# Attention of a two-layer decode-and-prompt kernel: 32-column tiles for the prompt's values, paged values and paged scores in one run

## The chip, the cores and the metric

One core of one Trainium2 chip. The time is that of one launch on the device, in microseconds (us); lower is better. A run's number is the time of one execution; three runs are given for the kernel before.

## The reference, cut to what matters

Two layers of a trunk over 1024 prompt tokens and 8 decoding sequences of 4 tokens each. Each layer projects, attends, gates, and then has a feed-forward part. The change touches the attention alone:

```python
def latent_attention(q_abs, q_pe, c_kv, k_pe, q_pos, k_pos, w_uv):
    s = (jnp.einsum('bqhc,bkc->bhqk', q_abs, c_kv)
         + jnp.einsum('bqhr,bkr->bhqk', q_pe, k_pe)) * ATTN_SCALE
    s = jnp.where((k_pos[None, :] <= q_pos[:, None])[None, None], s, NEG_INF)
    p = jax.nn.softmax(s, axis=-1)
    o_lat = jnp.einsum('bhqk,bkc->bqhc', p, c_kv)
    return jnp.einsum('bqhc,chv->bqhv', o_lat, w_uv)
# prompt: 8 blocks of 128 queries, 8 heads, keys up to the own block, 64 values per head
# sample: 8 sequences, each with 4096 cached (paged) positions of 128 latents + 32 rotary numbers,
#         plus its own 4 new positions
```

## The kernel before, in words

All engines run programs of their own that meet in counting semaphores. In each layer the attention is one loop over 64 "halves" `i`, written out on each engine. Half `i` is one head (`e = i % 2`) of job `k = i // 2`; `JOBS[k]` is a pair `(u, j)`: pair of heads `u`, query block `j` with `j + 1` key blocks of 128. For `u` = 0, 1, 2 the blocks come in the order 0, 7, 1, 6, 2, 5, 3, 4; for `u` = 3 as 4, 3, 5, 2, 6, 1, 7, 0. Four halves make a step `c = i // 4`, and `ph = i % 4` is the half within the step. "First half" is `ph` 0 and "third half" `ph` 2. A half with `j >= 4` is called big: its scores take two PSUM banks and its transposed probabilities two ring entries.

The prompt's part of a half, engine by engine:

- TensorE: `scores` of half `i + 2` into banks 0 to 3 (L2618, with the mask in L2621), `turn_p` transposes the normalised probabilities of half `i`, 128 columns at a time (L2630), and at the start of every second half `values(k - 1)` multiplies values by the transposed probabilities of the finished job (L2644), 64 columns of weights for each head, in bank 6.
- VectorE: `maxima` (L1898, the row maxima of the scores of half `i + 2`), `normalise` (L1904, L1907), `take_pt` (L1921, copies the second ring entry of a big half), `take_o` (L1914).
- ScalarE: `exps` (L1174), `take_pt` (L1187, copies the first ring entry of a half), `take_o` (L1181, the high part of the job's output).

One step of the paged part is laid between the four halves. Step `c` treats 512 cached positions of four sequences: `turn_keys` transposes the latents (L2665, two blocks in `ph` 0, two in `ph` 1; ScalarE L1193 and VectorE L1927 copy them out), VectorE's `take_ropes` (L1934) transposes the rotary keys, `step_scores` (L2676 in 32-column tiles, then L2678 over all columns) writes bank 7, VectorE's `step_max` (L1964) and ScalarE's `step_exp` (L1209) turn it into probabilities, `step_turn` transposes them (L2690), ScalarE's `step_pt` (L1216) copies them, `step_values` multiplies them with the latents (L2701, in 32-column tiles, bank 6), and VectorE's `step_out` (L1983) adds to the running sum. Every eighth step a short part for the new positions comes in (`new_scores`, `new_turn`, `new_values`, L2728). The latents arrive by SyncE's DMAs into three buffers, and a buffer's next DMAs wait for the `step_values` that read it.

The transposes go through a ring of two PSUM banks (4 and 5) in one order fixed by `ring_table`; entry `n` may be written when entry `n - 2` has been copied out (`evicted`), and ScalarE and VectorE must copy in that order too. The order on TensorE before is: `ph` 0: values, transposes, scores, keys, then `step_values(c - 1)`; `ph` 2: values, transposes, scores, then `step_scores(c)`; end of `ph` 3: `step_turn(c)`, except in the two steps for which `short(c)` holds, where it stands behind the next `values`. Because output of prompt and pages shares bank 6's first 128 columns, each writer of the bank waits for the readers of the one before (`o_new`, `do_free`).

## Time and profile before

| what | before |
|---|---|
| median of 3 runs | 2509.25 us (2505.19 to 2509.54) |
| profiled execution, first to last instruction | 2500.6 us |
| TensorE matmul busy | 2445.4 us, 98% |
| TensorE weight load busy | 2197.3 us, 88% |
| VectorE, ScalarE busy | 1527.6 us (61%), 1025.4 us (41%) |
| granted TensorE clock | 0.997 |

The profiled execution is known by its span alone, 2500.6 us; the median of the runs lies 8.65 us above it. A busy matmul engine in this profile is one with a matmul in its pipeline: a lone matmul of 128 columns counts 0.27 us, while in a stream the next starts 0.03 to 0.11 us after it. Time lost on TensorE therefore shows best in the distance between starts. Each fp32 matmul with real weights appears as two records, a transpose as one.

### The profile page before, as it was taken

The numbers are of one execution on the slowest core, as the hardware profiler recorded it, in microseconds if no ns is written. First come the engines' busy times: TensorE is split into PE (matmuls) and PEld (weight loads), VectorE is DVE, ScalarE is ACT, GpSimd is POOL, SyncE is SP. The second block draws the span as 40 slices with busy tenths as digits, with TensorE's granted clock in tenths as the row PEclk, the third lists the DMA queues.
The fourth block names the chain that finished last, engine by engine and source line by source line (L and its number), as shares of the span: only waits on it lengthen the run. The fifth ranks groups of instructions, "written<-read, shape, count | busy, mean of one in ns | idle before, by whom it ended". The sixth has DMA issues, their size and how long they took to land.

```text
span 2500.6 us, 47127 instructions
## 1 busy us (share of the span) xinstructions
PE 2445.4 (98%) x18500; PEld 2197.3 (88%) x18500; DVE 1527.6 (61%) x1986; ACT 1025.4 (41%) x1535; POOL 926.5 (37%) x395
## 2 busy tenths in 40 slices
PE   8999999999999999999999999999999999999998
PEld 6996666897999999999979966668989999999998
DVE  5546666348776557655674566663497675567646
ACT  3224555327533333433441246552274333333334
POOL 2331000122664666455213310002136654665451
PEclk9999999999999999999999999999999999999999
DMA  6114322314545544663431143222236356445644
GB/s 224 55 39 119 94 86 81 119 59 149 199 161 213 204 157 152 214 217 142 148 113 50 35 130 89 87 87 109 75 126 252 145 182 232 165 151 180 223 141 154
DMA packets 182347, 347.40 MB, mean 139 GB/s; under 512 B 33969, under 2 KB 46449, under 8 KB 181425
## 3 DMA queue, kind: packets, MB, share of 16 engines
q1 hardware_dynamic: 116128, 207.12, 24.9%
q10 hardware_dynamic: 63504, 129.77, 14.3%
q0 software_dynamic: 2560, 8.39, 1.2%
q8 instruction: 105, 1.72, 0.3%
q14 instruction: 50, 0.40, 0.1%
HBM read 292.94 MB, written 49.06 MB: 137 GB/s over the span
## 4 chain that ended last, share of the span: by engine, by line
PE 81%; DVE 7%; ACT 4%; POOLq 3%; issue 2%; DVEq 1%; DMA 1%; POOL 1%; SPq 0%; ACTq 0%
PE psum L2926 21%; PE psum L2973 20%; PE psum L2428 12%; PE psum L2618 4%; PE psum L2413 3%; PE psum L2644 3%; PE psum L2458 3%; PE psum L2630 2%; PE psum L2521 2%; PE psum L2665 2%; PE psum L2477 2%; PE psum L2381 1%; ACT z L1174 1%; PE psum L2488 1%; PE psum L2678 1%
## 5 line engine op out<-in xcount | busy, mean ns | idle before, releaser
L2973 PE MATMUL psum<-hidh,wh 128*128 128x264 f32 x1312 | 374.2, 285 | 8.4 <-issue 5.9
L2973 PE MATMUL psum<-hidl,wh 128*128 128x264 f32 x1312 | 373.6, 285 | 0.0
L2973 PE MATMUL psum<-hidh,wl 128*128 128x264 f32 x1312 | 372.7, 284 | 0.0
L2926 PE MATMUL psum<-hh,wh 128*128 128x264 f32 x1280 | 363.4, 284 | 0.1
L2926 PE MATMUL psum<-hh,wl 128*128 128x264 f32 x1280 | 362.8, 283 | 0.0
L2926 PE MATMUL psum<-hl,wh 128*128 128x264 f32 x1280 | 362.6, 283 | 0.0
L2134 DVE TENSOR_TENSOR z<-psum,z 128x528 f32<-128x528 f32 x336 | 226.9, 700 | 94.1 <-PE psum L2973 94.1
L2973 PEld LDWEIGHTS psum<-hidh,wh 128*128 128x128 f32 x1312 | 246.5, 188 | 10.4 <-issue 7.0
L2973 PEld LDWEIGHTS psum<-hidh,wl 128*128 128x128 f32 x1312 | 247.2, 188 | 0.0
L2973 PEld LDWEIGHTS psum<-hidl,wh 128*128 128x128 f32 x1312 | 246.9, 188 | 0.0
L2926 PEld LDWEIGHTS psum<-hh,wh 128*128 128x128 f32 x1280 | 240.5, 188 | 0.5 <-issue 0.5
L2926 PEld LDWEIGHTS psum<-hh,wl 128*128 128x128 f32 x1280 | 240.6, 188 | 0.0
L2926 PEld LDWEIGHTS psum<-hl,wh 128*128 128x128 f32 x1280 | 240.5, 188 | 0.0
L2428 PE MATMUL psum<-hh,wh 128*128 128x352 f32 x720 | 234.7, 326 | 0.1
L2428 PE MATMUL psum<-hh,wl 128*128 128x352 f32 x720 | 231.4, 321 | 0.0
L2428 PE MATMUL psum<-hl,wh 128*128 128x352 f32 x720 | 231.0, 321 | 0.0
L792 POOL TENSOR_TENSOR wh<-raw,ones 128x1024 fp32r<-128x1024 f32 x36 | 72.3, 2007 | 347.2 <-PE psum L2428 259.4
L808 POOL TENSOR_TENSOR wl<-raw,wh 128x1024 fp32r<-128x1024 f32 x42 | 108.3, 2579 | 181.3 <-ACT wh L1354 178.3
L904 POOL DMA_INDIRECT z<-cache_k,krows x32 | 30.5, 954 | 379.5 <-DVE cn L1934 375.2
L2124 DVE TENSOR_TENSOR hidl<-z,hidh 128x1056 fp32r<-128x1056 f32 (+1 forms) x100 | 159.1, 1591 | 10.4 <-ACT hidh L1340 10.4
L808 POOL TENSOR_TENSOR wl<-sacc,wh 128x1024 fp32r<-128x1024 f32 x38 | 92.3, 2428 | 146.8 <-ACT wh L1354 127.7
L2428 PEld LDWEIGHTS psum<-hh,wh 128*128 128x128 f32 x720 | 135.1, 188 | 2.1 <-DVE hl L1709 0.7
(329 smaller groups left out, 5935.0 us busy)
## 6 DMA issues: line engine op xcount, KB each, us to landing
hh<-h_quarters ACTq DMA_DIRECT2D x60, 1056.0 KB, 5.4
hl<-h_quarters ACTq DMA_DIRECT2D x60, 1056.0 KB, 7.5
raw<-wst SPq DMA_DIRECT2D x48, 512.0 KB, 3.6
z<-cache_c SPq DMA_DIRECT2D x352, 64.0 KB, 1.8
x<-x_spill SPq DMA_DIRECT2D x4, 4224.0 KB, 14.5
sacc<-wst SPq DMA_DIRECT2D x56, 256.0 KB, 3.2
t<-wst SPq DMA_DIRECT2D x56, 256.0 KB, 3.0
cn<-wst SPq DMA_DIRECT2D x56, 256.0 KB, 3.9
```

Of the source, the lines that this page charges most:

```text
L792: pool.tensor_tensor(wh[:, s, :], src, ones[:, 0:1].to_broadcast([P, TW]), ALU.mult)
L808: pool.tensor_tensor(wl[:, s, :], src, wh[:, s, :].bitcast(F32), ALU.subtract).then_inc(split.sem, 1)
L2124: dve.tensor_tensor(hid_of(t, hidl)[:, ks, :], src[:, ks, :], hid_of(t, hidh)[:, ks, :].bitcast(F32), ALU.subtract).then_inc(hid_l.sem, 1)
L2134: dve.tensor_tensor(part, dn_banks(u), part, ALU.add).then_inc(dn_free.sem, 1)
L2413: ins = pe.matmul(bank3(u, g), w, m[:, k, cols(g)], start=(first and n == 0), stop=(last and n == 2))
L2428: ins = pe.matmul(bank3(u, g), w[:, s, o:o + P], m[:, k, cols(g)], start=(k == 0 and n == 0), stop=(k == kk - 1 and n == 2))
L2458: ins = pe.matmul(bank, u_w[w], m[:, k, cols(g)], start=(first and n == 0), stop=(last and n == 2))
L2477: ins = pe.matmul(bank3(u, g), nxt[u][:, k * P:k * P + P], x[:, k, cols(g)], start=(k == 0), stop=(k == KD - 1))
L2618: ins = pe.matmul(ps[2 * e + h][:, 0:w], qs[e][0:KQ, u, tok(j)], keys[0:KQ, 2 * (u % 2) + e, 512 * h:512 * h + w], start=True, stop=not last)
L2644: ins = pe.matmul(ps[6][64 * e:64 * e + 64, 0:P], vals[:, kb, (2 * u + e) * VD:(2 * u + e) * VD + VD], pts[2 * e + kb // 4][:, kb % 4, :], ...
L2926: ins = pe.matmul(psum[:, up_bank(st, u) + q, 0:HW], w[:, o:o + P], m[part], start=(fresh and k == 0 and n == 0), stop=(k == 3 and n == 2) ...
L2973: ins = pe.matmul(psum[:, 2 * u + q, 0:HW], w[:, o:o + P], m[:, t, k * HB + q * HW:k * HB + q * HW + HW], start=(fresh and k == 0 and n == ...
```

## The change

It does four things.

- `values` uses four 32-column tiles where it had two of 64; twice as many matmuls, each half as wide in its weights.
- Prompt output, paged output and the output for the new positions get columns of their own in bank 6 (`prompt_o`, `paged_o`, `new_o`), so TensorE no longer waits for `o_new` or `do_free` before `step_values`, and ScalarE's `take_o` waits in the third half for the paged values' end before it reads the bank. The new positions' probabilities get a place of their own (`ptn`).
- On TensorE the third half now starts with `values`, `step_values(c - 1)`, (`new_values`) and `step_scores(c)` in one run, ahead of the half's transposes and scores. On VectorE the third half's order becomes `normalise(i + 1)`, `take_o`, `step_out(c - 1)`, `step_max(c)`, `take_pt(i)`, `maxima(i + 2)`.
- `step_turn(c - 1)` always stands in the first half, behind `values`; `short` is gone. The ring's entry for it and ScalarE's `step_pt` move with it.

```diff
--- before.py
+++ after.py
@@ -103,6 +103,8 @@
     for i in range(HALVES):
         ph, c = i % 4, i // 4
         big = JOBS[i // 2][1] >= 4
+        if ph == 0 and c > 0:
+            order.append((("x", c - 1), "act"))
         order.append((("p", i, 0), "act"))
         if big:
             order.append((("p", i, 1), "dve"))
@@ -115,7 +117,8 @@
         if ph == 3:
             if i in K_AT:
                 order.append((("k",) + K_AT[i], "act" if K_AT[i][1] == 0 else "dve"))
-            order.append((("x", c), "act"))
+            if c == STEPS - 1:
+                order.append((("x", c), "act"))
             if c == CHUNKS:
                 order.append((("f", 0), "act"))
     table, done = [], {"act": 0, "dve": 0}
@@ -268,6 +271,7 @@
         ptd = cnf[:, 512:1024].rearrange("p (r n) -> p r n", r=4)
         oacc = [zf[:, 9856:9984], cnf[:, 1024:1152]]
         olat = [cnf[:, 1152:1280], zf[:, 0:128]]
+        ptn = olat[0][0:NS, :]
         cks = [f.rearrange("p (b r c) -> p b r c", b=QB, r=4)
                for f in (zf[:, 4224:6272], raw[:, :, :].rearrange("p s n -> p (s n)"), zf[:, 6784:8832])]
         tab = rinv[0:1, 512:768].bitcast(I32).rearrange("o (n q) -> o n q", q=4)
@@ -279,6 +283,7 @@
 
         psum = ctx.enter_context(nc.psum_tensor("psum", [P, 8, 512], F32))
         ps = [psum[:, i, :] for i in range(8)]
+        prompt_o, paged_o, new_o = ps[6][:, 0:P], ps[6][:, P:2 * P], ps[6][:, 2 * P:3 * P]
 
         S = {}
 
@@ -1178,7 +1183,9 @@
 
                     u, j = JOBS[k]
                     act.wait_ge(o_full.sem, at.value(o_full, k + 1))
-                    act.activation(hh[:, u, tok(j)], ps[6][:, 0:P], ACT.Copy).then_inc(o_hi.sem, 1)
+                    if k % 2 == 0:
+                        act.wait_ge(do_full.sem, at.value(do_full, out_of_step(k // 2) - 1))
+                    act.activation(hh[:, u, tok(j)], prompt_o, ACT.Copy).then_inc(o_hi.sem, 1)
 
                 def take_pt(i):
 
@@ -1200,7 +1207,7 @@
 
                 def new_pt(quad):
                     turned(("n", quad))
-                    act.activation(ptd[0:NS, 0, :], ring_bank(("n", quad))[0:NS, 0:P], ACT.Copy).then_inc(t_act.sem, 1)
+                    act.activation(ptn, ring_bank(("n", quad))[0:NS, 0:P], ACT.Copy).then_inc(t_act.sem, 1)
 
                 def step_exp(c):
 
@@ -1248,6 +1255,8 @@
                         exps(i + 1)
                     if i % 2 == 0 and k > 0:
                         take_o(k - 1)
+                    if ph == 0 and c > 0:
+                        step_pt(c - 1)
                     take_pt(i)
                     if ph == 0:
                         take_keys(c, 0)
@@ -1264,7 +1273,8 @@
                         step_exp(c)
                         if i in K_AT and K_AT[i][1] == 0:
                             more_keys(K_AT[i][0])
-                        step_pt(c)
+                        if c == STEPS - 1:
+                            step_pt(c)
                         if c == CHUNKS:
                             turned(("f", 0))
                             act.activation(olat[0], ring_bank(("f", 0))[:, 0:P], ACT.Copy).then_inc(t_act.sem, 1)
@@ -1911,7 +1921,7 @@
 
                     u, j = JOBS[k]
                     dve.wait_ge(o_hi.sem, at.value(o_hi, k + 1))
-                    dve.tensor_tensor(hl[:, u, tok(j)], ps[6][:, 0:P], hh[:, u, tok(j)].bitcast(F32),
+                    dve.tensor_tensor(hl[:, u, tok(j)], prompt_o, hh[:, u, tok(j)].bitcast(F32),
                                       ALU.subtract).then_inc(o_new.sem, 1)
 
                 def take_pt(i):
@@ -1954,7 +1964,7 @@
                     dve.wait_ge(dexp.sem, at.value(dexp, first))
                     dve.tensor_copy(stat[:, 23:24], stat[:, 14:15])
                     dve.wait_ge(do_full.sem, at.value(do_full, first))
-                    dve.tensor_copy(oacc[quad], ps[6][:, 0:P]).then_inc(do_free.sem, 1)
+                    dve.tensor_copy(oacc[quad], new_o).then_inc(do_free.sem, 1)
                     dve.drain()
 
                 def step_max(c):
@@ -1981,12 +1991,13 @@
                     quad = c // CHUNKS
                     dve.wait_ge(do_full.sem, at.value(do_full, out_of_step(c)))
                     dve.scalar_tensor_tensor(out=oacc[quad], in0=oacc[quad], scalar=stat[:, 6 + s:7 + s],
-                                             in1=ps[6][:, 0:P], op0=ALU.mult, op1=ALU.add).then_inc(do_free.sem, 1)
+                                             in1=paged_o, op0=ALU.mult, op1=ALU.add).then_inc(do_free.sem, 1)
                     dve.drain()
                     if c % CHUNKS == CHUNKS - 1:
                         dve.reciprocal(stat[:, 22:23], stat[:, 23:24])
                         dve.drain()
                         dve.tensor_scalar(oacc[quad], oacc[quad], stat[:, 22:23], None, ALU.mult).then_inc(on_new.sem, 1)
+                        dve.drain()
 
                 gate_low(NB)
                 dve.wait_ge(vs_out.sem, at.value(vs_out, 16))
@@ -2007,11 +2018,17 @@
                 for i in range(HALVES):
                     k, ph, c = i // 2, i % 4, i // 4
                     big = JOBS[k][1] >= 4
+                    if ph == 2:
+                        normalise(i + 1)
                     if i % 2 == 0 and k > 0:
                         take_o(k - 1)
+                    if ph == 2:
+                        if c > 0:
+                            step_out(c - 1)
+                        step_max(c)
                     if big:
                         take_pt(i)
-                    if i + 1 < HALVES:
+                    if ph != 2 and i + 1 < HALVES:
                         normalise(i + 1)
                     if ph == 0 and c > 0:
                         take_ropes(c)
@@ -2022,13 +2039,9 @@
                             take_ropes(c)
                     if i + 2 < HALVES:
                         maxima(i + 2)
-                    if ph == 0:
-                        if c > 0:
-                            step_out(c - 1)
-                        if c % CHUNKS == 0:
-                            new_max(c // CHUNKS)
+                    if ph == 0 and c % CHUNKS == 0:
+                        new_max(c // CHUNKS)
                     if ph == 2:
-                        step_max(c)
                         if c % CHUNKS == 0:
                             new_out(c // CHUNKS)
                     if ph == 3:
@@ -2641,10 +2654,10 @@
                     pe.wait_ge(do_free.sem, at.value(do_free))
                     for kb in range(j + 1):
                         for e in range(2):
-                            ins = pe.matmul(ps[6][64 * e:64 * e + 64, 0:P],
-                                            vals[:, kb, (2 * u + e) * VD:(2 * u + e) * VD + VD],
-                                            pts[2 * e + kb // 4][:, kb % 4, :], start=(kb == 0), stop=(kb == j),
-                                            skip_group_check=True, tile_position=(0, 64 * e))
+                            for v in (64 * e, 64 * e + 32):
+                                ins = pe.matmul(prompt_o[v:v + 32, :], vals[:, kb, 2 * u * VD + v:2 * u * VD + v + 32],
+                                                pts[2 * e + kb // 4][:, kb % 4, :], start=(kb == 0), stop=(kb == j),
+                                                skip_group_check=True, tile_position=(0, v))
                     ins.then_inc(o_full.sem, 1)
                     at.step(o_new)
 
@@ -2678,10 +2691,6 @@
                     pe.matmul(ps[7][:, :], qrd[:, quad, :], rtt, start=False, stop=True,
                               skip_group_check=True).then_inc(ds_full.sem, 1)
 
-                def short(c):
-
-                    return c < STEPS - 1 and JOBS[2 * c + 1][1] + JOBS[2 * c + 2][1] < 7
-
                 def step_turn(c):
 
                     pe.wait_ge(dexp.sem, at.value(dexp, c + c // CHUNKS + 2))
@@ -2694,11 +2703,9 @@
 
                     s = c % CBUFS
                     evicted(RING_AT["x", c])
-                    pe.wait_ge(o_new.sem, at.value(o_new))
-                    pe.wait_ge(do_free.sem, at.value(do_free))
                     for r in range(4):
                         for b in range(QB):
-                            ins = pe.matmul(ps[6][rows_of(b), 0:P], ptd[:, r, rows_of(b)], cks[s][:, b, r, :],
+                            ins = pe.matmul(paged_o[rows_of(b), :], ptd[:, r, rows_of(b)], cks[s][:, b, r, :],
                                             start=(r == 0), stop=(r == 3), skip_group_check=True,
                                             tile_position=(0, 32 * b))
                     ins.then_inc(do_full.sem, 1)
@@ -2724,8 +2731,7 @@
 
                 def new_values(quad):
                     evicted(RING_AT["n", quad])
-                    pe.wait_ge(o_new.sem, at.value(o_new))
-                    pe.matmul(ps[6][:, 0:P], ptd[0:NS, 0, :], cn[0:NS, NB, 0:CL], start=True,
+                    pe.matmul(new_o, ptn, cn[0:NS, NB, 0:CL], start=True,
                               stop=True).then_inc(do_full.sem, 1)
                     at.step(do_free)
 
@@ -2774,8 +2780,14 @@
                     next_big = i + 2 < HALVES and JOBS[k + 1][1] >= 4
                     if i % 2 == 0 and k > 0:
                         values(k - 1)
-                    if ph == 0 and c > 0 and short(c - 1):
+                    if ph == 0 and c > 0:
                         step_turn(c - 1)
+                    if ph == 2:
+                        if c > 0:
+                            step_values(c - 1)
+                        if c % CHUNKS == 0:
+                            new_values(c // CHUNKS)
+                        step_scores(c)
                     turn_p(i, 0)
                     if i + 2 < HALVES:
                         scores(i + 2, 0)
@@ -2789,18 +2801,12 @@
                         scores(i + 2, 1)
                     if ph == 0:
                         turn_keys(c, 1)
-                        if c > 0:
-                            step_values(c - 1)
                         if c % CHUNKS == 0:
                             new_scores(c // CHUNKS)
                     if ph == 1:
                         turn_keys(c, 3)
                         if c % CHUNKS == 0:
                             new_turn(c // CHUNKS)
-                    if ph == 2:
-                        step_scores(c)
-                        if c % CHUNKS == 0:
-                            new_values(c // CHUNKS)
                     if ph == 3:
                         if i in K_AT:
                             u, h = K_AT[i]
@@ -2812,7 +2818,7 @@
                             pe.wait_ge(exped.sem, at.value(exped, HALVES))
                             pe.wait_ge(gate_l.sem, at.value(gate_l, NB + 1))
                             out_part(0, (4, 5, 6, 7))
-                        if not short(c):
+                        if c == STEPS - 1:
                             step_turn(c)
                         if c == CHUNKS:
                             pe.wait_ge(on_new.sem, at.value(on_new, 1))
@@ -2825,6 +2831,8 @@
                 evicted(len(RING) - 2)
                 evicted(len(RING) - 1)
                 out_part(1, (4, 5))
+                pe.wait_ge(o_new.sem, at.value(o_new))
+                pe.wait_ge(do_free.sem, at.value(do_free))
                 step_values(STEPS - 1)
                 out_part(1, (6, 7))
                 pe.wait_ge(on_new.sem, at.value(on_new, 2))
```

## Rows read from the trace of the kernel before

**Rows 1.** The page: busy time, share of the span, instructions.

```profile
PE 2445.4 (98%) x18500; PEld 2197.3 (88%) x18500; DVE 1527.6 (61%) x1986; ACT 1025.4 (41%) x1535; POOL 926.5 (37%) x395
```

**Rows 2.** Busy time by stretch, us and instructions: the first layer's attention.

```profile
core 0: us, PE busy (x) PEld busy (x) DVE busy (x) ACT busy (x) POOL busy (x), PEclk, DMA share, GB/s
215.00:465.00 250.00, 241.97 (x2139) 160.87 (x2138) 162.10 (x385) 144.42 (x350) 12.31 (x13) 1.00 0.30 88
```

**Rows 3.** Timeline of step 6, third half to values: start, us, engine, line.

```profile
321.18 0.38 PE L2630 MATMUL psum<-cst,z 128*128 128x128 f32 x2
...
321.49 1.07 PE L2676 MATMUL psum<-z,sacc 128*32 128x512 f32 x8
321.60 0.43 DVE L1921 COPY t<-psum 128x256 f32<-128x256 f32 x1 [0.40 <-PE psum L2630]
...
322.17 0.62 DVE L1907 TENSOR_SCALAR z<-z,stat 128x768 f32<-128x768 f32 x1
322.49 1.13 PE L2678 MATMUL psum<-cn,sacc 128*128 128x512 f32 x2
322.71 0.68 DVE L1898 TENSOR_REDUCE stat<-psum 128x1 f32<-128x512 f32 x1
...
323.43 0.69 ACT L1174 ACTIVATE z<-psum,stat 128x512 f32<-128x512 f32 x1 [2.06 <-DVE stat L1898]
323.45 0.60 PE L2630 MATMUL psum<-cst,z 128*128 128x128 f32 x4
...
323.89 1.02 PE L2618 MATMUL psum<-scratch,free_b 96*128 96x512 f32 x2
...
324.11 0.59 ACT L1187 ACTIVATE t<-psum 128x512 f32<-128x512 f32 x1
...
324.81 0.38 PE L2630 MATMUL psum<-cst,z 128*128 128x128 f32 x2
...
325.23 0.42 DVE L1921 COPY t<-psum 128x256 f32<-128x256 f32 x1 [0.66 <-PE psum L2630]
...
325.44 0.66 PE L2690 MATMUL psum<-cst,z 128*128 128x128 f32 x4 [0.25 <-ACT z L1209]
...
326.03 1.53 PE L2644 MATMUL psum<-t,scratch 128*64 128x128 f32 x24
```

**Rows 4.** Timeline behind those values.

```profile
327.49 0.66 PE L2630 MATMUL psum<-cst,z 128*128 128x128 f32 x4
```

**Rows 5.** Timeline around the paged values of step 4.

```profile
299.30 0.60 PE L2665 MATMUL psum<-cst,z 128*128 128x128 f32 x4
...
299.83 1.08 PE L2701 MATMUL psum<-raw,cn 128*32 128x128 f32 x32
...
300.85 0.44 PE L2630 MATMUL psum<-cst,z 128*128 128x128 f32 x2
```

**Rows 6.** Timeline at the end of step 7, one of the two short ones.

```profile
338.48 0.30 PE L2630 MATMUL psum<-cst,z 128*128 128x128 f32 x1
...
338.81 0.29 DVE L1921 COPY t<-psum 128x128 f32<-128x128 f32 x1
...
339.43 0.19 PEld L2644 LDWEIGHTS psum<-t,scratch 128*64 128x64 f32 x3 [0.85 <-ACT t L1187]
```

**Rows 7.** TensorE's waits of the whole run; one wait of step 4.

```profile
PEld psum L2690 <- ACT z L1209: 13.9, 26, 0.8
PEld psum L2630 <- DVE z L1907: 7.5, 16, 1.4
...
292.09 0.42 PEld L2630 LDWEIGHTS psum<-cst,z 128*128 128x128 f32 x4 [1.40 <-DVE z L1907]
```

**Rows 8.** Timeline of step 6, second half: a copy and the key transpose behind it.

```profile
316.83 0.49 ACT L1187 ACTIVATE t<-psum 128x384 f32<-128x384 f32 x1
...
318.36 0.42 PEld L2665 LDWEIGHTS psum<-cst,z 128*128 128x128 f32 x4
```

**Rows 9.** Timeline of step 12, second half: the same pair.

```profile
409.64 0.59 ACT L1187 ACTIVATE t<-psum 128x512 f32<-128x512 f32 x1
...
410.28 1.09 PE L2665 MATMUL psum<-cst,z 128*128 128x128 f32 x8 [0.29 <-ACT t L1187]
```

## The prediction, made before the changed kernel was seen

> **What bounds the kernel now.** I read the page first: the matmul engine shows 98% of the span, VectorE 61%, ScalarE 41% [rows 1]. Nearly all of the gain or loss must be time on TensorE. The change touches only the attention, so I then took the first layer's attention by stretch: TensorE 242.0 of 250 us, VectorE 162.1, ScalarE 144.4, clock at its full level of 2.4 GHz [rows 2]. The second layer's is the same program. "Busy" hides small losses here, because a matmul of 128 columns counts 0.27 us while the next may start 0.11 us later. So I read the timeline by distances between starts. In a stream of transposes it is 0.11 us ((0.60 - 0.27) / 3 of the four records at 323.45 [rows 3]); anything longer is a mode switch or a wait.
>
> In step 6 the order of events is [rows 3]: the last third-half transposes at 321.18, the paged scores 321.49 to about 323.45, then the fourth half's transposes and scores, a wait for ScalarE, the paged transposes at 325.44, the values at 326.03. TensorE is in a stream throughout except for one wait of 0.41 us: the two transposes at 324.81 leave it free at 325.03, and the next starts at 325.44. So TensorE sets the pace, but its neighbours are close behind: the copy that the values need ended at 325.65 (325.23 + 0.42), 0.38 us before they started. What lies between a transposition and the values that use it is therefore not spare.
>
> **Gains, both layers.**
>
> *Mode switches.* Full to 32-column tiles: the last of the four key transposes starts at 299.63, the first paged value matmul at 299.83, 0.203 us instead of 0.110 [rows 5]. Into and out of the 64-column tiles it is the same: 1.53 us for 24 records puts the last start at 327.29, the next is at 327.49 [rows 3, 4]. I price a switch at 0.093 us. The third half had four switches besides the one inside the paged scores (in and out of values, into the scores), the paged values two in the first half. In one run, two of the former vanish in each of 16 steps and both of the latter in 15, less two where the new positions' scores stay; 60 a layer, 120 x 0.093 = 11.2 us.
>
> The Trainium skill ("TensorEngine Tiling (Array Packing)", Key Properties) says that changing the tiling mode drains the engine. Read as a full drain of 0.27 us, a switch would cost 0.163 us more than a stream and 120 of them 19.6 us; the sum below would end 8 us lower. The trace shows 0.093, before the last matmul's end, so I keep that.
>
> *Narrower values.* A 64-column record takes (1.53 - 0.27) / 23 = 54.8 ns [rows 3], a 32-column one (1.08 - 0.27) / 31 = 26.1 ns [rows 5]. A key block needs 4 of the former (219 ns) or 8 of the latter (209 ns): 144 blocks a layer, 288 x 0.0104 = 3.0 us. The four tiles run side by side just as the two did; no stream is halved.
>
> *Waits that go.* The paged transposes waited for the exponential. Summed over weight loads this is 13.9 us in 26 places [rows 7], but a weight load may start early; by distances between starts, as above, I get 0.41 us in step 6 and between 0 and 0.66 in the others, 6.7 in all (bounds 3.5 and 13.9). Both short steps of a layer wait before the values: the last transpose could be followed at 338.68 by a switched stream, the load starts at 339.43 [rows 6]; 4 x 0.78 = 3.1. In step 4 the fourth half's transposes wait for `normalise` [rows 7]; it now stands first on VectorE. That and its like in step 0 give about 2.6. Together 12.4 us.
>
> Gains: 11.2 + 3.0 + 12.4 = 26.6 us.
>
> **Costs, both layers.**
>
> *The values of every second job, at the head of the first half.* This is the large term. `step_scores` stood between the score matmuls of the next step's first half and the fourth half; `step_turn` stood between the fourth half's transposes and the values. Both covers go. What the values need is the fourth half's first ring entry, copied by ScalarE, and ScalarE copies it behind `exps` of the next half, which waits for VectorE's `maxima`, which stands behind `take_pt` of the third half. From the end of the third half's last transpose (321.56) that chain costs, in durations of rows 3: copy 0.35 (0.43, with 0.08 overlapped), maxima 0.68, exponential 0.68 (323.43 to 324.11), copy 0.59, and three hand-overs of 0.04: 2.42 us. TensorE's own work until the values is what ran from 323.45 to 325.03, 1.58 us, counted from 0.16 us before that end, plus one switch of 0.09: 1.51 us. So it stands 0.9 us. Then come the remaining waits in front of `values`: in step 7 the copy ends at 339.10 and the load starts at 339.43 [rows 6], 0.33 us later, where a single wait costs 0.05 (the exponential's in rows 3). I take 0.2: 1.1 us.
>
> From the other side: the short steps already lack `step_turn` in front of the values and wait 0.78 us with only one block to copy in the second entry (0.29 us); with four blocks, 0.39 more. VectorE's copy alone thus gives 0.78 to 1.17 us. In steps 0, 4 and 8 the third half has eight blocks, its `normalise` ends late and pushes `step_max` and the copy back; there I estimate 1.4 to 1.5. In the steps where keys are made in the fourth half that matmul waits instead of the values, for the same entry. For the last pair of heads, whose third halves are small, the same chain from the maxima gives about 0.95. Average 1.1, bounds 0.78 and 1.5. Fifteen boundaries a layer: 30 x 1.1 = 33 us. This replaces the two kinds of waits counted above as gone.
>
> *The second half.* Without the paged values (1.02 + 0.09 = 1.11 us of TensorE, rows 5) in the first half, the key transposes reach their ring entry sooner. In step 6 the copy ends at 317.32 and the fourth key transposition starts at 318.36: slack 1.04, lost 1.11 [rows 8]. Steps with fewer blocks in the third half have less slack; I estimate 0.1 to 0.4 us, 11 steps a layer at 0.17: 3.8 us. In steps 12 to 15 there is no slack: the copy ends at 410.23, the transposes start at 410.28 after 0.46 us of waiting [rows 9], and the chain behind it (copy, normalise, the rotary transposition, maxima, exponential, copy) starts at the first half's transposes, which the run does not delay. The full 1.11 is lost: 8 x 1.1 = 8.8 us (bounds 4 and 9). `new_values` now stands ahead of the scores and waits for its copy: 2 x 0.5 = 1.0.
>
> Costs: 33 + 3.8 + 8.8 + 1.0 = 46.6 us. Costed at nothing: `step_exp` in the fourth half (the paged transposes come two blocks of work later); ScalarE's extra wait in `take_o` (its next copy belongs to transposes that come after the run anyway); the gathers, which are released by `step_values` two halves later but have a step and a half left before use. If that cover failed, the first key transposes of a step would wait for a DMA.
>
> **The sum.** 46.6 - 26.6 = +20.0 us on 2500.6, so a span of 2520.6. The runs' median is 8.65 above the span: 2529.
>
> **Rivals.**
>
> 1. *The copies come in time*: faster. Place: the wait before the values at the head of the first half. With no wait there the sum is 13.6 - 26.6 = -13.0 (2496); with 0.2 us each, -7 (2502). It decides at 0.43 us a boundary. For it: VectorE and ScalarE are a third idle [rows 2], and both have less queued behind the run. Against it: idle engines do not shorten a chain of latencies, and rows 6 show 0.78 with more cover. 0.13.
>
> 2. *Nothing measurable*, the same wait at 0.3 to 0.55 us: 0.08.
>
> 3. *The chain grows*: `step_max` and `step_out` hold VectorE up in most steps as in steps 0, 4, 8, so that a boundary costs 1.5 us: +12 us more, 2541. For it: the paged scores' last matmul counts 0.6 us after its start and VectorE must wait for it. Against it: in steps with seven blocks or fewer the next transposes and scores cover this. 0.11.
>
> 4. *Narrow tiles stream faster*: 13 ns a record instead of 26 would save 288 x 0.104 = 30 us more, 2499. Rows 5 show 26.1 with the same moving width. 0.01. The Trainium skill ("TensorEngine Tiling (Array Packing)", Theoretical Speedup) lists up to 2x for 64 and up to 4x for 32, which taken for the prompt's values would say this; here the narrower tile also halves the work of each matmul.
>
> 5. The forecast, 0.67.
>
> **How the numbers follow.** About 0.2% (5 us) is what a measurement of this kernel tells from no change. Faster: rivals 1 and 4, 0.14. Same: 0.08. Slower: the rest, 0.78. The forecast's own bounds (0.78 to 1.5 us a boundary, 4 to 9 in the last steps) reach from 2515 to 2541. To leave out no more than 2 in 10 the range takes in rival 2, the edge of rival 1 and rival 3 with some spread: 2504 to 2545.
>
> **What the changed profile would show.** Right: the first values matmul of each first half stands idle about 1 us behind ScalarE L1187 or VectorE L1921; the wait for the exponential before the paged transposes is gone; values, paged values and paged scores follow each other at 0.03 us; VectorE's key-side waits in steps 12 to 15 grow. Wrong: idle time before those values under 0.4 us; or a wait on the gathers; or a 32-column run of a hundred records that streams slower than 26 ns, which would add to the loss instead.

## The result and the profile after

The changed kernel takes 2529.59 us (median of 4, 2528.96 to 2530.73) against 2507.22 us before (4, 2501.65 to 2509.54): ratio 1.0088, 95% interval 1.0074 to 1.0102. It is slower by 22 us. The forecast was 2529 us.

The page after, to be read beside [rows 1], and the first layer's attention by stretch, beside [rows 2] (the stretch is 10 us longer, because the attention is):

```profile
PE 2437.0 (96%) x19652; PEld 2204.6 (87%) x19652; DVE 1531.3 (61%) x1986; ACT 1024.6 (41%) x1535; POOL 923.6 (37%) x395
```

```profile
core 0: us, PE busy (x) PEld busy (x) DVE busy (x) ACT busy (x) POOL busy (x), PEclk, DMA share, GB/s
215.00:475.00 260.00, 236.29 (x2701) 161.96 (x2700) 162.85 (x384) 143.74 (x349) 12.23 (x13) 0.99 0.31 86
```

VectorE and ScalarE do what they did. TensorE is busy for less time (236.3 instead of 242.0 us), but it stands 23.7 us idle instead of 8.0. The granted clock was 0.99 of full after and 1.00 before. So the loss is waiting, and the question is for what.

I measure the attention of a layer as the distance between the first transposition of its first half and that of its last. Before, it is 241.62 and 242.28 us, 483.90 in both layers; after, 252.42 and 252.09, 504.51. That is +20.6 us. The groups of the transposition line after, by source line, show the two ends roughly (the last half's block itself is included):

```profile
L2643 PE MATMUL psum<-cst,z x288: 270/273/468, 221.8 to 474.3; 128*128 128x128 f32 x144
...
L2643 PE MATMUL psum<-cst,z x288: 270/273/468, 1474.7 to 1726.7; 128*128 128x128 f32 x144
```

The waits of the weight loads over the whole run (us in total, times, longest), which answer to [rows 7]:

```profile
PEld psum L2658 <- ACT t L1194: 24.8, 22, 1.4
...
PEld psum L2579 <- ACT t L1194: 8.9, 8, 1.2
...
PEld psum L2643 <- ACT cn L1223: 7.0, 6, 1.9
...
PEld psum L2643 <- DVE t L1931: 2.9, 4, 0.9
```

The paged transposition's 13.9 us behind the exponential have shrunk to 0.9 us in four places. In their place stand 24.8 us before the prompt's values (22 places) and 8.9 us before the key-making matmul (8 places), both for the copy `take_pt`: together 30 places, the 30 boundaries of the forecast. The third row, 7.0 us in six places, was not forecast: the first half's own transposes wait for a ring entry that `step_pt` has not copied yet. The fourth, 2.9 us in four places, is in the fourth half of steps 0 and 4, where the transposes wait for VectorE's copy.

Step 6 after, in the timeline (start, us, engine, line), beside [rows 3, 4]:

```profile
321.23 0.86 PE L2658 MATMUL psum<-t,scratch 128*32 128x128 f32 x24
...
321.91 1.06 PE L2708 MATMUL psum<-z,cn 128*32 128x128 f32 x32
...
322.78 1.04 PE L2689 MATMUL psum<-z,sacc 128*32 128x512 f32 x8
...
323.75 1.12 PE L2691 MATMUL psum<-cn,sacc 128*128 128x512 f32 x2
...
324.71 0.60 PE L2643 MATMUL psum<-cst,z 128*128 128x128 f32 x4
...
326.50 0.42 DVE L1931 COPY t<-psum 128x256 f32<-128x256 f32 x1 [0.55 <-PE psum L2643]
...
326.84 0.68 DVE L1908 TENSOR_REDUCE stat<-psum 128x1 f32<-128x512 f32 x1
...
327.55 0.69 ACT L1179 ACTIVATE z<-psum,stat 128x512 f32<-128x512 f32 x1 [1.60 <-DVE stat L1908]
327.65 0.39 PE L2643 MATMUL psum<-cst,z 128*128 128x128 f32 x2
...
328.08 0.42 DVE L1931 COPY t<-psum 128x256 f32<-128x256 f32 x1 [0.56 <-PE psum L2643]
...
328.23 0.59 ACT L1194 ACTIVATE t<-psum 128x512 f32<-128x512 f32 x1
...
329.02 1.52 PE L2658 MATMUL psum<-t,scratch 128*32 128x128 f32 x48 [0.98 <-ACT t L1194]
...
330.47 0.66 PE L2699 MATMUL psum<-cst,z 128*128 128x128 f32 x4
```

The forecast chain can be read off: copy of the third half 326.50, maxima 326.84, exponential 327.55, ScalarE's copy 328.23 to 328.82, values 329.02. TensorE's last transpose before them starts at 327.76 (327.65 + 0.11); a switched stream would have started the values at 327.96. The wait is 1.06 us.

### The profile page after: what moved, and what is told of

It is laid out like the page before. It is cut to its first block, busy times and chain, and to the rows that moved or that the text cites. A ratio compares the mean times of both kernels' runs of the same rounds, so it can differ in the third digit from the quotient of the medians.

```text
span 2527.2 us, 49433 instructions
## 1 busy us (share of the span) xinstructions
PE 2437.0 (96%) x19652; PEld 2204.6 (87%) x19652; DVE 1531.3 (61%) x1986; ACT 1024.6 (41%) x1535; POOL 923.6 (37%) x395
## 4 chain that ended last, share of the span: by engine, by line
PE 79%; DVE 8%; ACT 4%; issue 3%; POOLq 2%; DVEq 1%; POOL 1%; DMA 1%; SPq 0%; ACTq 0%
PE psum L2934 20%; PE psum L2981 19%; PE psum L2441 12%; PE psum L2471 3%; PE psum L2426 3%; PE psum L2631 3%; PE psum L2658 2%; DVE stat L1908 2%; PE psum L2534 2%; ACT z L1179 2%; PE psum L2490 2%; PE psum L2678 1%; PE psum L2643 1%; PE psum L2394 1%; PE psum L2691 1%
```

## The experiments

For each, "attention" is the sum over both layers as above (before 483.9, after 504.5). Outside the attention the profiled runs spread over 2016.7 to 2028.1 us, in kernels that are the same there. So a difference of a few microseconds between two spans is read from the attention. It is that of one profiled execution for each kernel; its two layers agree within 0.8 us in every kernel.

### e1: only the narrower values, in the kernel before

```diff
-                            ins = pe.matmul(ps[6][64 * e:64 * e + 64, 0:P],
-                                            vals[:, kb, (2 * u + e) * VD:(2 * u + e) * VD + VD],
+                            for v in (64 * e, 64 * e + 32):
+                                ins = pe.matmul(ps[6][v:v + 32, 0:P], vals[:, kb, 2 * u * VD + v:2 * u * VD + v + 32],
...
-                                            skip_group_check=True, tile_position=(0, 64 * e))
+                                                skip_group_check=True, tile_position=(0, v))
```

> The kernel before with the prompt's values in 32-column tiles and nothing else. Measured over the two attention stretches (first transposition of half 0 to that of half 63; 483.9 us together before, 504.5 in the changed kernel). Theory (the order costs, the tiles give a little): 3.0 us less, about 481, no new wait. Rival (twice as many value matmuls cost issue time or instruction loading): 484 or more, a 32-column record slower than 26 ns in the long streams.

Measured: 2508.14 us, ratio 0.9989 (0.9978 to 1.0000), attention 484.39. Most steps became 0.01 to 0.03 us shorter. Step 8 rose by 0.7 us in the first layer, in the wait before `new_turn`, and by 0.5 in the second. So the sum rose by 0.5 us where 3.0 less was expected. A narrow record takes 26.5 ns in a long stream (1.245 us for the 47 intervals of 48 records) where the wide one takes 54.8. Two narrow for one wide gain 1.8 ns, not the 2.6 that I had taken from the short run of [rows 5]. And a block of values has one more interval to pay, since the hand-over behind it stays at 0.203 us: 24 wide records took 1.258 us from first to last, 48 narrow ones 1.245. Over 32 steps this is about 1 us.

### e2: the changed kernel with the 64-column values back

```diff
-                            for v in (64 * e, 64 * e + 32):
-                                ins = pe.matmul(prompt_o[v:v + 32, :], vals[:, kb, 2 * u * VD + v:2 * u * VD + v + 32],
...
+                            ins = pe.matmul(ps[6][64 * e:64 * e + 64, 0:P],
+                                            vals[:, kb, (2 * u + e) * VD:(2 * u + e) * VD + VD],
...
```

> The changed kernel with 64-column tiles for the prompt's values; the order is kept. Theory: slower than the changed kernel by 3.0 us of stream and one more switch in each of 32 third halves (0.093 less the hand-over within the run, 1 to 3 us): stretches about 509. Rival (the narrow tiles cost): below 504.

Measured: 2534.06 us (one run), attention 506.99, so +2.5 (+4 to +6 was expected). Steps 0 to 14 rose by 3.6 us together, up to 0.17 each, and the last step fell by 0.5 and 0.6; why it fell no experiment shows. Within the run, equal tiles are worth little: one switch saved a step, and a part of that comes back at the hand-over (last section).

### e3: the paged scores back behind the third half

```diff
                             new_values(c // CHUNKS)
-                        step_scores(c)
                     turn_p(i, 0)
...
+                    if ph == 2:
+                        step_scores(c)
```

VectorE's `step_max` goes back behind `maxima` with them.

> The changed kernel with the paged scores back at the end of the third half (VectorE's step_max behind maxima again); values and paged values still run together at its head. Theory (the values at the head of the first half lost their cover): the wait before them, 0.8 to 1.2 us at 30 boundaries and 29.6 us in all, falls to near nothing, two switches in each of 32 steps come back (5 to 6 us): stretches about 480, 20 to 24 below the changed kernel. Rival (the moved paged transposition is what uncovers the values): the wait stays over 0.6 us a boundary, stretches about 500.

Measured: 2519.84 us, ratio 1.0038 (1.0024 to 1.0052), attention 491.87: 12.6 us less than the changed kernel, not the 20 to 24 expected. The wait vanished in steps 12 to 14 and in three of the four that make keys (5, 8, 9), but stayed in step 4 (0.84 us) and in seven others a layer. Step 6 of this kernel in the timeline shows who ends it now:

```profile
320.59 1.12 PE L2691 MATMUL psum<-cn,sacc 128*128 128x512 f32 x2
...
322.19 0.60 ACT L1194 ACTIVATE t<-psum 128x512 f32<-128x512 f32 x1 [0.36 <-PE psum L2643]
...
322.91 0.38 PE L2643 MATMUL psum<-cst,z 128*128 128x128 f32 x2
...
323.33 0.42 DVE L1931 COPY t<-psum 128x256 f32<-128x256 f32 x1 [0.66 <-PE psum L2643]
...
324.12 1.52 PE L2658 MATMUL psum<-t,scratch 128*32 128x128 f32 x48 [0.83 <-DVE t L1931]
```

ScalarE's copy is in time (322.79), as I had argued. VectorE's copy of the second entry is not: it can't start before the two transposes just ahead of the values end. From the last of these starts (323.02) to the values it takes 1.10 us, of which 0.20 is a stream. This floor of 0.9 us has nothing to do with the scores: it stands in e7 and e10 too, where they are at their old place. The paged transposition used to hide it, and it is what moving the transposition costs wherever the second entry has nothing else behind it. The scores' part is what went: between nothing and 0.2 us in steps 1 to 3, 6, 7 and 10, 0.35 in step 11, and the whole 0.9 to 1.2 in steps 5, 8 and 9 and in steps 12 to 14. In step 0 the wait even grew (1.16 to 1.47 us). And 4.8 of the 12.6 us went elsewhere, in the fourth half's transposes of steps 0, 4, 3 and 7 (see the section on why the prediction was right).

### e4: e3, and the paged transposition home as well

```diff
-                        if c == STEPS - 1:
+                        if not short(c):
                             step_turn(c)
```

with its ring entry and `step_pt` back in the fourth half.

> As e3, and the paged transposition back at the end of the fourth half as before. Theory: the wait for the exponential returns (6.7 us by distances before), the ring waits of the last pair of heads behind the paged entry go (some 5 us): stretches within 3 us of e3. Rival (moved transposition is the loss): 15 us or more below e3.

Measured: 2513.99 us, ratio 1.0019 (1.0009 to 1.0028), attention 487.98: 3.9 us below e3, a little more than the 3 expected; the rival's 15 is far off. What is left of the change here (values run behind each other, narrow tiles, regions of their own, `normalise` first) still stands 4 us above the kernel before. By steps it gains in the plain ones (14.77 and 14.74 us in steps 2 and 6 for 14.98 and 14.95) and loses in steps 12 to 15 (16.54, 16.18, 16.12, 11.64 for 15.42, 15.38, 15.41, 11.19), where the second half was already short of TensorE work; its key transposes wait 1.28 us in step 12, for 0.46 before.

### e10: the opposite, only the paged transposition moved

```diff
-                    if ph == 0 and c > 0 and short(c - 1):
+                    if ph == 0 and c > 0:
                         step_turn(c - 1)
```

in the kernel before, with the ring entry and `step_pt` moved along.

> The kernel before with the paged transposition behind the first half's values, its ring entry and ScalarE's copy moved with it as in the change, and nothing else (in e7 ScalarE's copy stayed ahead of the next exps and held it up). Theory: in steps 1, 2, 6 and 10 a wait of about 0.9 us for VectorE's copy takes the place of 0.4 us for the exponential, so these are 0.4 to 0.5 us longer than before; steps 3 and 7 as before; steps with key making and steps 12 to 15 within 0.3 us: stretches 486 to 491 against 483.9. Rival (moving the transposition is most of the change's loss): 497 or more, as e7.

Measured: 2511.66 us (one run), attention 489.22, +5.3, inside the 486 to 491 expected. Steps 1, 2, 6 and 10 lose 0.45 us each in the first layer, as expected. Steps 14 and 15 lose 0.8 and 0.9, against the 0.3 expected, and step 8 gains 0.9: a wait of 0.92 us between the paged transposition and an extra one that this step has is gone. This kernel has the unforecast wait too, by the weight loads' list:

```profile
PEld psum L2636 <- ACT cn L1219: 5.3, 6, 1.5
```

So it comes from the transposition's new place and not from the run. The floor of e3 can be read here by size: from the last transpose to the values it takes 0.99, 1.10, 1.23 and 1.365 us where VectorE copies one, two, three and four blocks (steps 3, 6, 1, 0). The changed kernel has 0.99, 1.26, 1.42 and 1.365 there, so in these steps the chain over maxima and exponential adds at most 0.2 us to what VectorE's copy takes by itself.

### e6: ScalarE copies before the next exponential

```diff
-                    if 0 < i < HALVES - 1:
+                    if 0 < i < HALVES - 1 and ph != 3:
                         exps(i + 1)
...
                     take_pt(i)
+                    if i < HALVES - 1 and ph == 3:
+                        exps(i + 1)
```

In the changed kernel, this takes maxima and exponential out of the chain in front of the values.

> The changed kernel with one thing other on ScalarE: in the fourth half take_pt stands ahead of the next half's exps. Theory (the values wait for the copy behind exps): the wait before the values of the first half falls from about 1.05 to about 0.85 us where the third half has six or seven blocks (there VectorE's copy of the second entry comes next), and to 0.3 or less at steps 12 to 15, where there is no second entry; stretches 8 to 11 us below the changed kernel's 504.5. Rival (VectorE alone sets the wait): less than 3 us.

Measured: 2518.37 us (one run), attention 496.62, 7.9 us below the changed kernel, at the edge of the 8 to 11 expected. In step 6 the same floor appears as in e3:

```profile
323.38 0.38 PE L2645 MATMUL psum<-cst,z 128*128 128x128 f32 x2
...
323.79 0.42 DVE L1933 COPY t<-psum 128x256 f32<-128x256 f32 x1 [0.56 <-PE psum L2645]
...
324.58 0.86 PE L2660 MATMUL psum<-t,scratch 128*32 128x128 f32 x24 [0.82 <-DVE t L1933]
```

The distance from the last transpose to the values fell from 1.257 to 1.097 us and no further. In steps 12 to 14 the wait was gone, but steps 13 and 14 grew all the same (17.26 and 18.20 us for 16.94 and 17.93): the first half's second group of transposes now waits 1.13 and 1.65 us where it waited 0.25 and 1.10, behind the later exponential.

### e7: the transposition behind the values, but its copy at the old place

```diff
-                    return c < STEPS - 1 and JOBS[2 * c + 1][1] + JOBS[2 * c + 2][1] < 7
+                    return c < STEPS - 1 and c != CHUNKS
```

in the kernel before.

> The kernel before with its paged transposition always behind the first half's values (except at step 8), nothing else of the change. Theory: the wait for the exponential goes (6.7 us) and a wait before the values comes in its place, for VectorE's copy, of 0.7 to 0.9 us in the steps without key making, with no other cover lost: stretches 482 to 490 against 483.9. Rival (this move is the loss of the change): 495 or more.

Measured: 2518.77 us (one run), attention 497.13. A miss by 7 us, and the number of the rival (495 or more). But the wait before the values is the one of e10 (1.10 us from the last transpose in step 6). ScalarE's `step_pt` stayed ahead of the next exponentials and had to wait for a transposition that TensorE now did behind the values, so the exponentials came late: the first half's key transposes of steps 12 to 15 waited 0.9 to 1.35 us, where before they waited 0.1 to 1.05. The moved operation must take its copy with it; that is why e10 costs 5 us and this one 13.

### e8: the paged values back in the first half

```diff
                     if ph == 0:
                         turn_keys(c, 1)
+                        if c > 0 and home(c - 1):
+                            pe.wait_ge(o_new.sem, at.value(o_new))
+                            pe.wait_ge(do_free.sem, at.value(do_free))
+                            step_values(c - 1)
```

in the changed kernel, for every step.

> The changed kernel with the paged values back behind the first half's key transposes; values and paged scores still run together at the head of the third half. Theory: the waits of key transposes and ring in the first and second half fall by the cover of 1.11 us, mostly in steps 12 to 15 (about 8 us), two switches of 0.093 in 30 steps come back (5.6 less two hand-overs of 0.06 each): stretches 2 to 8 us below 504.5, the steps 12 to 15 down by 0.8 each, the others up by 0 to 0.1. Rival (the wait before the values is all of the loss): no step falls.

Measured: 2525.06 us (one run), attention 505.58, +1.1: wrong in sign. Steps 12 to 14 fell by 0.83, 0.78 and 0.74 as expected, so the second half there does miss the paged values. Steps 1, 2, 5, 6, 9 and 10 rose by about 0.5 (step 0 by 0.7 and 0.2, steps 3, 7 and 11 by 0.15 or less, while 4 and 8 fell a little), and the timeline of step 6 shows more in it than two switches:

```profile
321.67 0.86 PE L2665 MATMUL psum<-t,scratch 128*32 128x128 f32 x24
321.77 0.60 ACT L1205 ACTIVATE z<-psum 128x512 f32<-128x512 f32 x1 [1.75 <-PE psum L2685]
...
322.62 0.64 PE L2696 MATMUL psum<-z,sacc 128*32 128x512 f32 x4
```

The paged scores need the step's last keys, whose copy ends at 322.37. With the paged values in front of them, that wait was covered; directly behind the prompt's values the scores come some 0.3 us late, and 0.5 in steps 1, 5 and 9.

### e9: back to the late order where it is better, by step

Transposition home in all steps, scores at the head in steps 0 to 3, 6, 7 and 10 with `step_exp` ahead of `exps`, and paged values home from step 11 on:

```diff
+                    if ph == 3 and head(c):
+                        step_exp(c)
                     if 0 < i < HALVES - 1:
                         exps(i + 1)
```

> A mixture meant to beat both: the paged transposition at the end of the fourth half as before; in steps 0 to 3, 6, 7 and 10 paged scores at the head of the third half with ScalarE's step_exp ahead of exps (it should fit in while ScalarE waits for the maxima); elsewhere paged scores at the end; paged values at home from step 11 on. Theory (cover in front of the values is what counts): the wait there falls to 0.4 to 0.5 us in those seven steps, each about 0.3 us shorter than before; stretches 477 to 482, against 483.9 before. Rival (the exponential delays exps and the chain with it): the seven steps are as long as in the changed kernel, stretches 484 or more.

Measured: 2511.19 us, ratio 1.0015 (1.0004 to 1.0026), attention 485.12: 3 us above the 477 to 482 expected, and in the rival's range (484 or more). The seven steps with the scores at the head are about as long as in the changed kernel. The exponential of the paged scores was early now, but the transposition then waited 0.87 to 1.26 us for the ring entry that `take_pt` frees, because that copy stood behind both exponentials.

### e11: e9 with the copy between the exponentials

```diff
+                    if ph == 3 and head(c):
+                        step_exp(c)
+                    if 0 < i < HALVES - 1 and not (ph == 3 and head(c)):
                         exps(i + 1)
...
                     take_pt(i)
+                    if ph == 3 and head(c):
+                        exps(i + 1)
```

with the scores at the head in steps 0 to 11.

> Meant to beat both. As the changed kernel in steps 0 to 11 with two things other: the paged transposition at the end of the fourth half as before, and ScalarE's order there is step_exp, take_pt, exps; steps 12 to 15 as before. In e9 the transposition waited for the ring entry that take_pt frees behind exps; in e6 the values waited 0.9 us for VectorE's copy with nothing in front. Theory: both go, what is left before the values is 0.3 us; steps 1, 2, 6, 10 at 14.3 to 14.6 us against 14.9 to 15.1 before, stretches 472 to 478 against 483.9, the run some 8 us faster than before. Rival (a later exps uncovers the next chain, or step_exp is too late in ScalarE's order): a new wait at the first half's transposes, stretches 482 or more.

Measured: 2502.41 us against 2507.61, ratio 0.9982 (0.9971 to 0.9992), attention 479.27. It beats both kernels, by 5.2 us and by 27, but is short of what was expected (8 us faster, attention 472 to 478). Its steps 1, 2, 6 and 10 take 14.69, 14.47, 14.47 and 14.52 us (before, steps 1, 2 and 6: 15.09, 14.98, 14.95), at or above the upper end of the 14.3 to 14.6 expected; step 8 even grew, from 18.03 to 18.47. Step 6:

```profile
324.39 0.69 ACT L1223 ACTIVATE z<-psum,stat 128x512 f32<-128x512 f32 x1
...
325.33 0.60 ACT L1201 ACTIVATE t<-psum 128x512 f32<-128x512 f32 x1
...
325.95 0.69 ACT L1186 ACTIVATE z<-psum,stat 128x512 f32<-128x512 f32 x1
326.06 0.38 PE L2657 MATMUL psum<-cst,z 128*128 128x128 f32 x2
...
326.28 0.60 PE L2717 MATMUL psum<-cst,z 128*128 128x128 f32 x4
...
326.48 0.42 DVE L1940 COPY t<-psum 128x256 f32<-128x256 f32 x1 [0.56 <-PE psum L2657]
...
327.26 1.52 PE L2672 MATMUL psum<-t,scratch 128*32 128x128 f32 x48 [0.39 <-DVE t L1940]
```

Paged exponential, copy, next exponential, in this order on ScalarE. The transposition (L2717) stands again between the last two transposes and the values, and of the 0.9 us floor 0.46 is left by the distance between starts. The three-part run is kept, and what it saves is kept with it.

## Why the prediction was right

The moves can be put in a row by their attention time: before 483.9; transposition moved (e10) 489.2; with the values run, narrow tiles and regions (e3) 491.9; with the scores at the head (the change) 504.5. The two moves that took the covers from the values cost 5.3 and 12.6 us. The values standing uncovered is the mechanism of the forecast, and most of both costs. Its terms, measured by distances between starts, both layers:

- **Wait before the values at the head of the first half**: forecast 33 us at 1.1 each, measured 29.8, and 2.6 more one place earlier. In the first layer, less the distance that a stream would have: 1.16, 1.22, 1.05 and 0.79 in steps 0 to 3, 0.9 to 1.2 where keys are made, 1.05 and 0.88 in steps 6 and 7, 1.05 and 0.86 in steps 10 and 11, 0.88 to 0.94 in steps 12 to 14. In steps 0 and 4 VectorE's copy is late behind `step_max`, as forecast, but it is the fourth half's own transposes that wait for it, 0.43 and 0.86 us in each layer. Step 4:

```profile
294.14 0.69 DVE L1931 COPY t<-psum 128x512 f32<-128x512 f32 x1
...
294.88 0.66 PE L2643 MATMUL psum<-cst,z 128*128 128x128 f32 x4 [0.70 <-DVE t L1931]
```

  With it these two steps wait 1.6 and 1.8 us (forecast 1.4 to 1.5), and step 8, where the forecast expected the same, only 0.92. Averaged over 30 boundaries this is 1.08 us, so rival 1 (copies in time), rival 2 (0.3 to 0.55 us) and rival 3 (1.5 us) fall. One thing in the forecast's derivation was off: the chain over maxima and exponential was priced as what the values wait for. e3 and e10 show that in steps 0 to 3, 6, 7 and 10 VectorE's copy alone gives a wait of 0.8 to 1.16 us, which was the forecast's own second estimate, and that the chain ends at most 0.2 us behind it. In steps 5, 8, 9 and 12 to 14, where e3 removed the wait, the chain alone sets it.
- **Second half** (key transposes): forecast 3.8 + 8.8, measured 8.5 in all, about 2 in steps 0 to 11 and 6.5 in the last four. e8 shows its size in steps 12 to 14: about 0.8 us each, not 1.1.
- **The ring**: not in the sum at all, measured 6.7 us (0.25, 1.10 and 1.89 us in steps 13, 14 and 15 of the first layer). This is the step that failed: of the moved transposition I had counted what it no longer covers, and not who waits for the ring entry behind it. In steps 13 to 15 ScalarE reaches `step_pt` only behind a long exponential and `take_o`; the first half's second group of transposes waits. The timeline after, at the last step:

```profile
461.56 1.11 ACT L1179 ACTIVATE z<-psum,stat 128x1024 f32<-128x1024 f32 x1 [1.06 <-DVE stat L1908]
...
462.66 0.27 ACT L1188 ACTIVATE hh<-psum 128x128 fp32r<-128x128 f32 x1
...
462.82 0.60 ACT L1223 ACTIVATE cn<-psum 128x512 f32<-128x512 f32 x1
...
463.47 0.66 PE L2643 MATMUL psum<-cst,z 128*128 128x128 f32 x4 [1.73 <-ACT cn L1223]
```

  Together with the waits before the values and of the key transposes, this is why steps 12 to 15 carry 7.7 of the 10.8 us that the first layer's attention grew by (15.42, 15.38, 15.41, 11.19 us before; 16.88, 16.94, 17.93, 13.40 after). Steps 4, 5 and 9 lost 0.64 to 0.69 us each, and the plain steps 1 to 3 only 0.1 to 0.2.
- **The fourth half of steps 3 and 7**: not in the sum either, 2.2 us. Its first transposes wait 0.55 us for ScalarE's copy of the ring entry before; the paged scores used to stand there, and in e3, where they stand there again, the wait is gone.
- **Mode switches**: forecast 11.2, measured some 16.7, about 0.5 us a step. Step 6 shows it: it grew by 0.12 us (14.95 to 15.07) while its waits grew by 0.64 (0.41 before the paged transposition gone, 1.05 before the values come), so everything else fell by 0.52, 0.03 of it by the narrow tiles. Over both layers everything else fell by 17.7 us. The price of 0.093 us holds. More of it comes back because the paged values, lifted out of the stream of transposes, take both of their hand-overs with them: 0.203 us ahead and 0.203 behind are replaced by one of 0.110; and the paged values and the paged scores each take 0.024 us less from first to last start (0.808 to 0.784, 1.530 to 1.505). Against that, the hand-overs within the run cost 0.089 us instead of the 0.03 foreseen. e2 shows the smallness of the run's own part. The full drain of 0.27 us a switch, which the Trainium skill ("TensorEngine Tiling (Array Packing)", Key Properties) could be read to say, would have given 19.6; no run here shows that: a change of mode took 0.203 us from start to start wherever nothing else was waited for.
- **Narrow tiles**: forecast 3.0, measured about 1 (e1). Rival 4 falls: e1 alone would have gained 30 us by it.
- **Waits that go**: forecast 12.4, measured 12.5; but the wait for `normalise` in steps 0 and 4 came back one group of transposes later, in the 2.6 us above. Not in the sum is the wait of 0.92 us in step 8 that e10 showed to go with the transposition's move: 1.8 us.
- **New positions**: forecast 1.0 for `new_values`, measured next to nothing (0.1 us in step 0). Around `new_turn`, in the second half, 1.4 us of waiting came instead.
- **The gathers**: costed at nothing; in the whole run one key transposition waited 0.6 us for one.

Costs 29.8 + 2.6 + 8.5 + 6.7 + 2.2 = 49.8, and some 4 us in smaller ones (1.6 around the new positions, 0.6 between the key-making matmuls, 1.8 as a spacing of 0.10 to 0.15 us more between records in the second half of the last step); gains 16.7 + 1 + 12.5 + 1.8 = 32.0. That makes +22, where the two attentions show +20.6: the sum of many small distances is good to about 1 us. The forecast's +20.0 has the right mechanism, but that it came so close is in part luck. Costs were missing (6.7, 2.2 and about 3 of the 4) and the narrow tiles gained 2 less; against them the hand-overs gained 5.5 more, step 8 gained 1.8, and the second half cost 4.1 less.

The base was wrong as well. I had put 8.65 us above the span, from the median against one profiled span. The run that was profiled after took 2528.96 us by its own time with a span of 2527.2, so only 1.8 us lie around a span. Of the other 6.9 us, 6 came from outside the attention (2022.65 us after, 2016.70 before). The ten other kernels, unchanged there, have 2017.7 to 2028.1, so the profiled run of before was a short one in that part. The hit within 1 us owes something to that luck; the medians differ by 22.4 us, the forecast's terms by 20.

What stays open: the spacing in the last step, which e2, e3 and e8 do not have and e6 has, is not explained. The ring term and the waits before the values act on each other in steps 13 to 15 (e6 took away the one and the other grew), so their split there is a reading of distances, not an experiment. What would become of steps 12 to 15 with a further ring entry was not tried. Nor was the changed kernel run with its three-part run but without the regions of their own or with `normalise` at its old place, so these two parts of the change have no price of their own.

## What to carry to other kernels

When an operation is taken from between a transposition and its user, price what it covered: here a turn through PSUM, from transposition to copy to values, leaves 0.8 to 1.16 us by the size of the copy, although VectorE was busy for only 61% of the run, and this ate all that fewer mode switches gave. Follow every ring entry to its next user, and every moved copy to what it is queued behind; the same run gained once ScalarE's order was paged exponential, copy, next exponential. Take the changed part's time by distances between starts, since a span also carries several microseconds of the rest. And a sum that comes out right can hold wrong terms: here several misses of 2 to 7 us cancelled.

## What the runs showed of the hardware

- A hand-over between two streams of the same 32-column mode took 0.089 us from start to start (values to paged values, paged values to paged scores), not the 26 ns between two records of a stream. A change of mode took 0.203 us against 0.110 between two transposes.
- Two 32-column records cost nearly what one 64-column record costs (2 x 26.5 ns against 54.8 ns). The Trainium skill ("TensorEngine Tiling (Array Packing)", Theoretical Speedup) lists 2x and 4x for tiling; these concern small dimensions that leave the array empty, and in e1 the array was full in both forms.
- After the copy that they waited for had ended, the values began 0.20 us later in the changed kernel (328.82 to 329.02) and 0.37 us later in e3 (323.75 to 324.12), where the copy was VectorE's; 0.36 in e11 (326.90 to 327.26). The 0.33 us of [rows 6], from which I had taken part of the forecast's wait, is also behind a copy of VectorE's.
- From the last 128-column transpose to the values that use VectorE's copy of it took 0.99, 1.10, 1.23 and 1.365 us from start to start with one, two, three and four blocks in the copy (e10).
